# A one-core fp32r decoder layer: all SBUF buffers on multiples of 64 bytes, and the k-tiles of one operand 2112 bytes apart

## What is computed

```
xn = rmsnorm(x, mix_norm_g)
p  = xn @ w_in                                   # 1024 -> 10256 columns
ya, yb, yc, yd = mlstm(..), short_conv(..), mamba2(..), stick_breaking_attention(..)
lifted = einsum('bsie,ied->bsid', [ya,yb,yc,yd], w_lift)
merged = sum_i sigmoid(gates_i) * lifted_i
x = x + merged @ w_out
h = causal_dwconv(rmsnorm(x) @ w_up, conv_w) + conv_b      # 1024 -> 5632
x = x + (silu(h[:, :2816]) * h[:, 2816:]) @ w_down         # 2816 -> 1024
out = rmsnorm(x, final_norm_g)
```

## Time and profile before

| | |
|---|---|
| time, median of 3 runs | 1051.35 us (1050.12 to 1051.71) |
| span of the profiled execution, first to last instruction | 1048.9 us |
| TensorE (PE) busy | 1031.9 us, 98% |
| VectorE (DVE) busy | 593.3 us, 57% |
| ScalarE (ACT) busy | 424.8 us, 41% |
| GpSimd (POOL) busy | 67.7 us, 6% |
| HBM traffic | 103 GB/s over the span |

### The profile page before, as it was taken

How to read it: one execution, slowest core, us unless ns; L and a number is a source line. 1 busy time by engine, 2 the same in 40 slices (tenths; PEclk the granted TensorE clock), 3 DMA queues, 4 the chain that set the end, 5 groups by cost and what they waited for, 6 DMA issues and landing times.

```text
span 1048.9 us, 12635 instructions
## 1 busy us (share of the span) xinstructions
PE 1031.9 (98%) x4724; PEld 837.0 (80%) x4724; DVE 593.3 (57%) x764; ACT 424.8 (41%) x515; POOL 67.7 (6%) x74
## 2 busy tenths in 40 slices
PE   8999999999999999999999999989999999999996
PEld 6797888887777887777888888868888888888886
DVE  6834753766676576554454365687566566533323
ACT  5514446554435333434342334454444433423222
POOL 5610000000000000000000000400000000000002
PEclk9999999999999999999999999999999999999999
DMA  6331232223321333342242222413332232243312
GB/s 243 112 105 69 81 87 77 81 90 104 98 90 63 124 131 131 108 148 81 98 165 98 101 81 101 170 64 108 100 100 82 97 100 80 67 168 95 95 56 80
DMA packets 32024, 108.24 MB, mean 103 GB/s; under 512 B 3684, under 2 KB 5860, under 8 KB 31600
## 3 DMA queue, kind: packets, MB, share of 16 engines
q1 hardware_dynamic: 29520, 93.86, 27.1%
q0 software_dynamic: 2320, 13.69, 3.8%
q10 hardware_dynamic: 144, 0.14, 0.1%
HBM read 103.42 MB, written 4.25 MB: 103 GB/s over the span
## 4 chain that ended last, share of the span: by engine, by line
PE 93%; DVE 4%; ACT 2%; issue 1%; DMA 1%; DVEq 0%; SPq 0%; ACTq 0%
PE gb L411 81%; PE gb L444 4%; DVE w_lo L983 1%; PE xb L594 1%; PE gb L522 1%; PE xb L554 1%; PE xb L547 1%; PE xb L534 1%; PE xb L411 1%; ACT w_hi L699 1%; PE xb L511 1%; DMA raw<-w_stream 1%; DVE y_lo L991 1%; PE gb L462 1%; PE xb L582 0%
## 5 line engine op out<-in xcount | busy, mean ns | idle before, releaser
L983 DVE TENSOR_TENSOR w_lo<-raw,w_hi 128x1024 fp32r<-128x1024 f32 (+2 forms) x181 | 218.1, 1206 | 353.6 <-ACT w_hi L699 353.0
L699 ACT ACTIVATE w_hi<-raw 128x1024 fp32r<-128x1024 f32 (+2 forms) x181 | 183.8, 1017 | 424.9 <-PE gb L411 390.9
L411 PE MATMUL gb<-xn_hi,w_hi 128*128 128x512 f32 x720 | 285.7, 397 | 0.0
L411 PE MATMUL gb<-xn_lo,w_hi 128*128 128x512 f32 x720 | 282.1, 392 | 0.0
L411 PE MATMUL gb<-xn_hi,w_lo 128*128 128x512 f32 x720 | 280.7, 390 | 0.0
L411 PE MATMUL gb<-y_hi,w_hi 128*128 128x512 f32 x400 | 160.8, 402 | 5.4 <-DVE y_lo L991 3.7
L411 PEld LDWEIGHTS gb<-xn_hi,w_hi 128*128 128x128 f32 x720 | 135.6, 188 | 31.3 <-issue 1.0
L411 PE MATMUL gb<-y_hi,w_lo 128*128 128x512 f32 x400 | 159.9, 400 | 0.0
L411 PEld LDWEIGHTS gb<-xn_lo,w_hi 128*128 128x128 f32 x720 | 135.6, 188 | 29.7 <-issue 1.4
L411 PE MATMUL gb<-y_lo,w_hi 128*128 128x512 f32 x400 | 159.0, 398 | 0.0
L411 PEld LDWEIGHTS gb<-xn_hi,w_lo 128*128 128x128 f32 x720 | 135.5, 188 | 29.4
(11 more groups left out here) (231 smaller groups left out, 1018.4 us busy)
## 6 DMA issues: line engine op xcount, KB each, us to landing
raw<-w_stream SPq DMA_DIRECT2D x149, 512.0 KB, 3.3
raw<-w_down SPq DMA_DIRECT2D x16, 384.0 KB, 3.0
abc<-scr_a POOLq DMA_DIRECT2D x8, 640.0 KB, 4.2
raw<-w_down SPq DMA_DIRECT2D x16, 320.0 KB, 2.8
x_in<-xT SPq DMA_DIRECT2D x8, 256.0 KB, 6.2
x<-xT POOLq DMA_DIRECT2D x1, 2048.0 KB, 8.7
scr_x<-x POOLq DMA_DIRECT2D x1, 2048.0 KB, 7.4
x<-scr_x POOLq DMA_DIRECT2D x1, 2048.0 KB, 8.5
```

The costliest lines, as they stand in the source:

```text
L411: ins = pe.matmul(out, w[:, r, lo:hi], rhs(k)[x], start=(first and n == 0 and q == 0), stop=(last_ and n == len(ks) - 1 and q == 2))
L699: act.activation(w_hi[:, r, 0:n], raw[:, r, 0:n], ACT.Copy).then_inc(S["hi_ready"], 1)
L983: dve.tensor_tensor(w_lo[:, r, 0:n], raw[:, r, 0:n], w_hi[:, r, 0:n].bitcast(F32), ALU.subtract)\
```

## The change

`Map.put` rounds sizes up to 64 bytes instead of 32. And xn_hi and xn_lo get 16 more columns in each k-tile, which are never used, so that their k-tiles start 2112 = 33 x 64 bytes apart instead of 2048. All else is as it was, and each engine's instructions are the same ones in the same order.

```diff
         def put(self, name, shape, dt=F32):
             size = 4 * int(np.prod(shape[1:]))
             t = at(name, shape, dt, self.at)
-            self.at += (size + 31) // 32 * 32
+            self.at += (size + 63) // 64 * 64
             return t
 
     m = Map(base)
     raw = m.put("raw", [P, RING, 1024])
     w_hi = m.put("w_hi", [P, RING, 1024], F32R)
     w_lo = m.put("w_lo", [P, RING, 1024], F32R)
-    xn_hi = m.put("xn_hi", [P, KD, T], F32R)
-    xn_lo = m.put("xn_lo", [P, KD, T], F32R)
+    xn_hi = m.put("xn_hi", [P, KD, T + 16], F32R)[:, :, 0:T]
+    xn_lo = m.put("xn_lo", [P, KD, T + 16], F32R)[:, :, 0:T]
```

## The result

The changed kernel takes 1055.24 us (median of 5 runs, 1055.09 to 1056.69) where the kernel before took 1051.28 beside it. The ratio of the runs is 1.0044, 95% interval 1.0032 to 1.0056 (the two medians alone give 1.0038): slower by some 0.4%. The prediction said 1037.7 and faster. The number lies inside the stated range, the direction is wrong, and the case that came true is nearest to rival 1.

A forecast was written before the change was run, and what follows sets the result against it. TensorE, busy 98% of the span, bounds the kernel through its matmuls' start-to-start pace. Rounding's terms sum to 13.6 us and the spacing counts zero, taking 1051.35 to 1037.7 us; stated range 1033 to 1057.

The forecast's parts named there:

- rival 1: 64 bytes not enough, or moving and stationary must start alike modulo 128 to 512: xn slows, 1062 us; chance 0.22.
- The sum: Whole kernel: gains from y and h taking xn's pace of 0.2266 us a matmul add up to 13.6 us.
- input units 2 to 7: Input units with y moving: 144 matmuls each 0.0068 us faster, 1.0 us gained.
- lifts and lingering: 16 lift units (y) gain 2.8 us; slow pace lingering into the xn units behind them, 0.5 us.
- output projection: 8 units, half y and half xn: 192 matmuls go from 0.2322 to 0.2266 us, 1.1 us gained.
- up loop: Up units from the loop's third, half y and half xn: 912 matmuls each 0.0056 us faster, 5.1 us gained.
- down stage: Down stage with h moving: 462 matmuls each 0.0068 us faster, 3.1 us gained.
- the idle: TensorE's wait for y_lo at the up loop's head grows from 3.7 to some 4.2 us.
- (2): xn's k-tiles 2112 bytes apart, odd ones 64 above a multiple of 128: claimed no effect, 0.
- the 16 cycles: Difference between the paces of xn and of y and h, 0.0068 us at 2.4 GHz, matched to 64 bytes of fp32.
- unit 12: Unit with xn moving, weight slices 96 wide and 384 bytes apart, at 0.2317 us: xn's good address alone isn't enough.
- rival 2: Address or its distance to 64 not the cause: y, h and xn keep their paces, 1051.35 us; chance 0.17.

The follow-up runs named there:

- The mended kernel: The kernel before with sizes rounded up to 256 bytes instead of 32 and xn's k-tiles left 2048 bytes apart; 1037.23 us, ratio 0.9877.
- The sweep: No layer, TensorE alone: blocks of 48 matmuls, moving operand's place raised by 16 bytes against the weights; 226.7 ns a step at distance 0, 232.1 at 128.

## Why the prediction was wrong, point by point

- **What bounds the kernel**: right. The pace of the matmuls sets the end. The kernel before has two steady steps, 544 and 560 cycles, and the address sets them; other distances give steps between and above.
- **The sum**: right as a sum of what the fast pace is worth. The mended kernel has the terms: input units 2 to 7 0.9 us (said 1.0), units 13 to 96 3.0 (lifts and lingering, 3.3), output projection 1.05 (1.1), up loop 5.07 (5.1), down stage 3.09 (3.1), the idle 0.4 longer (0.5). Its span is 13.7 shorter, and the sum was 13.6. So what failed is not the price of the fast pace but the belief that this change brings it.
- **The step that failed** is "all stay on multiples of 64 ... I take zero for (2)", and with it "I take the distance of xn, 0.2266, as the new distance of y and h". The first term, 13.6 us for the rounding, came to 2.9: y and h stayed at 0.2333, and most of what was gained came from the mixed up loop and the 256-column matmuls, not from a fast y or h. The second, zero for the spacing, came to 5.5 us of loss: xn went from 0.2266 to 0.2317. The reason given was the 16 cycles, read as one further block of 64 bytes. The sweep shows that as a coincidence: a distance of 64 costs 5 or 6 cycles, 112 costs 11, 4 bytes cost 28. What the runs show in its place is that the step follows where the operand stands against the weights, modulo 256.
- **Rival 1** had the mechanism in its second half ("that moving and stationary start alike modulo 128 to 512") and unit 12 for it, and I gave it 0.22. It named a full price of 10.4 us; measured were 4.6 of span. xn went to 0.2317, not 0.2334 (6.0 us from unit 13 to the end of unit 96 instead of 9.1), the up loop lost 0.25 and not 1.1, and the 256-column matmuls, for which I had said 0 because two aligned and misaligned rows agreed at 0.120, gained 0.84. Those two rows were at distances 0 and 96, both bad for 256 columns.
- **The lingering** of the slow pace for some nine matmuls behind a switch, read from the earlier trace rows, is a start-up that depends on the case. Two blocks of the first sweep, both at distance 0 modulo 256, first and tenth start:

```profile
195.63 0.40 PE L65 MATMUL gb<-x_hi,w_hi 128*128 128x512 f32 x1
...
197.71 0.39 PE L65 MATMUL gb<-x_hi,w_hi 128*128 128x512 f32 x1
...
375.24 0.40 PE L65 MATMUL gb<-x_hi,w_hi 128*128 128x512 f32 x1
...
377.28 0.39 PE L65 MATMUL gb<-x_hi,w_hi 128*128 128x512 f32 x1
```

  The first follows a block at 240, itself a fast distance, and needs 2.08 us for nine; the second follows one at the slow distance 224 and needs 2.04, which is the steady 0.2267. So a slow start can come behind a fast distance and be missing behind a slow one. In the up loop of the kernel before, the xn half pays for it (0.2299 a step on average instead of 0.2267), and the y half too is above its steady pace (0.2346 instead of 0.2333).
- **The rule of 16-byte lines** (Trainium skill, "SBUF — State Buffer", Specifications (TRN2)), from which rival 2 took that nothing would change: distances of 16, 32, 48 bytes all lie on such lines, and the sweep has 231.7, 233.3, 233.3 against 226.7, so the measurement decides against that conclusion. The distances off 16 bytes neither bear the line out nor speak against it: 12 bytes (228.7) is faster than 16, and 4 bytes (238.3) slower. The Trainium skill, "TensorE: Matmul & The Clock Gate", Part 2, says that loading the next weights takes no read bandwidth from the running matmul, through a port of its own. In the sweep the pace depends by up to 3% on the weights' address while everything else is the same, which that sentence does not lead one to expect; that it is the weight load which hinders is not shown.

What stays open: whether two reads collide at all and, if so, which of the two weight tiles takes part, the one in use or the one being loaded; how long the start behind a switch lasts; and why the good distances are 0 and 240 at 512 columns and 112 and 192 at 256. The runs show the table and no model of it.

## What to carry to other kernels

When TensorE is the bound and runs 128x128 by 512 columns in fp32r with new weights for each matmul, put weights and moving operands at the same place modulo 256 bytes, and make the spacing of k-tiles a multiple of 256; then take the step in an undisturbed stretch as the check (544 cycles for 512 columns here, 560 where y and h stood). For 256 columns other distances are the good ones. Padding can make matmuls slower: 64 bytes between the k-tiles of one operand cost 0.5%. Two groups of operands with different paces in one trace are a question on everything by which they differ, their distance to a third buffer included, so a kernel that moves only one of the two is worth more than a fit to one number.

## What the runs showed of the hardware that was not expected

- The distance of moving operand and weights modulo 256 changes the pace of 512-column fp32r matmuls from 544 cycles (distances 0 and 240) to between 548 and 576; 128-column ones (0, 96, 192) and plain fp32 ones (0, 96) not at all.
- The best distances differ with the width: for 256 columns 112 and 192 bytes give 272 cycles where 0 gives 288.
- Changing the distance from tile to tile costs more than the mean of the steady steps: distances 0 and 128 in turn give 232.5 ns, where the two alone give 226.7 and 232.1.
- Behind a switch of distance the first nine or so matmuls can be slow even when both distances are fast (2.08 us for nine behind a block at 240) and can be fast at once behind a slow one (2.04 behind 224).
